# The last expert group of a two-layer transformer kernel: its filler matmuls set one matrix later, and its scatter split in two halves

## The chip, the cores and the metric

The kernel runs on one core of a Trainium2 chip. The metric is the device time of one launch in microseconds (us), lower is better. Everything is float32. A core has TensorE (PE, matmuls), VectorE (DVE), ScalarE (ACT), GpSimd (POOL) and SyncE (SP), which here issues the transfers.

## The reference

Two layers of a transformer on 256 tokens of width 1024. Each layer has an attention part (three branches, merged and projected) and a mixture of experts, and only the experts matter here:

```python
def hier_moe(h, w_grp, b_grp, w_router, b_router, w_gate, w_up, w_down):
    ...
        a = jnp.einsum('cd,edf->cef', t, w_gate)
        u = jnp.einsum('cd,edf->cef', t, w_up)
        hid = (jax.nn.silu(a) * u * combine[..., None]).astype(t.dtype)
        return jnp.einsum('cef,efd->cd', hid, w_down)
```

There are 32 experts of width 256, and a token uses two. The result is added to the residual x; the second layer is followed by a final normalization.

## The kernel before

**Stages.** Each layer is an attention block and a block of experts. The experts are handled in 8 groups of four. An expert has room for 32 tokens (`CAP`), so four experts fill the 128 columns of the array, each in its own strip of 32, and their four matmuls run side by side. An expert has three matrices of 1 MB each: gate, up and down. SyncE loads them one after another into a ring of 20 slots of SBUF, a load waiting only for the last reader of its slot.

**One group g in TensorE's program** (`moe_tensor`): `gate_up` (L1935) waits for the eight gate and up matrices of the group and issues its matmuls at L1947; `gather` (L1909, matmuls at L1919) collects the tokens of the next group; `turn_hidden` (L1979) transposes the hidden values, which ACT (L2080) and DVE (L2232, L2237) have made from the result of `gate_up` and which DVE takes back at L2245; `turn_weights` (L1971, L1976) transposes the selection weights, taken by ACT at L2084 into `ST`; `down` (L1985, L1996) multiplies by the down matrices, in two halves n of 512 output columns, into banks 5 and 6; ACT copies each half out of its bank into `ysb` (L2098); `scatter_group` (L2002, matmuls at L1954) adds the half of each expert's rows back to the tokens, in four accumulators in banks 0 to 3, one for each pair of token half t and column half.

**The end of a layer.** For the last two groups the order is another one: the down matrices of group 6 land behind the gate and up matrices of group 7, so `down` and `scatter_group` of group 6 stand behind `gate_up` and `turn_hidden` of group 7. Then come `turn_weights`, `down` and `scatter_group` of group 7. The down matrices of group 7 are loaded as halves (`down_half`, issued at L1803 and L1805 once `gate_up` of group 6 has read its slots, recorded as L594): first the four halves for n = 0, then the four for n = 1, and `down` of group 7 waits for the latter on the semaphore `s_side` (L1993). Each of the four last scatter sums is counted by `s_fin`, on which DVE adds it to the residual (L2255). In the second layer ACT then squares it for the final normalization (L807), and in the first layer the next attention block begins (its first matmuls are at L963).

**Fillers.** `keep_warm` (L596) issues matmuls of 128 columns on the identity, whose result nobody reads. A float32 matmul is two MATMUL records in the trace. In `gate_up` of the last group, twelve such fillers (`TAILWARM`, L49) stand between the wait for the sixth landed matrix (i = 5) and that for the seventh (i = 6):

```python
                pe.wait_ge(s_hde, g)
                for i in range(8):
                    if g == NGRP - 1 and i == 6:
                        keep_warm(pe, TAILWARM, bank[5])
                    moe_wait(pe, place(g, i))
```

TensorE works through its program in this order: a wait holds up everything behind it.

Of the kernel before, what the change touches and what calls it, by code (L numbers as in the profile page):

```python
# [39 lines left out]
NGRP = NE // 4  # L40
# [5 lines left out]
RING = 8  # L46
HROWS = 47
WARM, FILL = 14, 8
TAILWARM = 12  # L49
LOADS = 12 * NGRP  # L50


# [84 lines left out]
def program(nc, A, out, ctx):  # L137
# [195 lines left out]
    def csem(name):  # L333
        first[name] = sem(name)
        return first[name]
# [102 lines left out]
    s_hde = csem("expert_hiddenT_ready")  # L438
# [25 lines left out]
    def in_extra(c):  # L464

        return SLOTS < c < AHEAD
# [7 lines left out]
    def place(g, i):  # L474

        if g == NGRP - 1 and i < 8:
            return LOADS - 16 + i
        return 12 * g + i + (8 if g == NGRP - 2 and i >= 8 else 0)
# [9 lines left out]
    def moe_slot(c):  # L488

        assert c != SIDE and not in_extra(c)  # L490
        slot = PERM[turn_of(c)]
        g, i = item(c)
        if g and i < 8:
            other = PERM[turn_of(c ^ 1)]
            return max(slot, other) if c % 2 else min(slot, other)
        return slot
# [5 lines left out]
    def moe_home(c):  # L502

        return EXTRA[c - SLOTS - 1] if in_extra(c) else ring[:, moe_slot(c), :]
# [91 lines left out]
    def keep_warm(pe, n, b):  # L596

        for _ in range(n):
            pe.matmul(b[:, 0:P], ident, ident, start=True, stop=True)
# [210 lines left out]
    for layer in range(DEPTH):  # L810
# [5 lines left out]
        def moe_wait(eng, c):  # L816

            if c == SIDE:
                eng.wait_ge(s_part, PART + (layer + 1) * 64)
            elif in_extra(c):  # L820
                eng.wait_ge(s_side, layer * 96 + 32)
            else:
                eng.wait_ge(landed[moe_slot(c)], turns_moe[layer, c] * 16)
# [956 lines left out]
        def hidden_rows(g):  # L1780

            return hidT if g < NGRP - 1 else Sel[:, 0]
# [63 lines left out]
        def moe_tensor(pe):  # L1846
# [88 lines left out]
            def gate_up(g):  # L1935

                pe.wait_ge(s_hde, g)
                for i in range(8):
                    if g == NGRP - 1 and i == 6:
                        keep_warm(pe, TAILWARM, bank[5])  # L1940
                    moe_wait(pe, place(g, i))
                for k in range(KD):
                    if k % 4 == 0:
                        pe.wait_ge(s_xge, 2 * g + k // 4 + 1)
                    for e in range(4):
                        lo, hi = moe_slot(place(g, 2 * e)), moe_slot(place(g, 2 * e + 1))
                        last = pe.matmul(bank[4][CAP * e:CAP * e + CAP, :].rearrange("p (a f) -> p a f", a=2),  # L1947
                                         XT[:, k, CAP * e:CAP * e + CAP],
                                         ring[:, lo:hi + 1:hi - lo, k * F:(k + 1) * F],
                                         start=(k == 0), stop=(k == KD - 1))  # L1950
                last.then_inc(s_gu, 1)

            def scatter(g, t, half):
                return pe.matmul(bank[2 * t + half][:, :], ST[:, t * P:(t + 1) * P],  # L1954
                                 ysb[:, 512 * half:512 * half + 512], start=(g == 0), stop=(g == NGRP - 1),
                                 skip_group_check=True)
# [14 lines left out]
            def turn_weights(g):  # L1971
                pe.wait_ge(s_sw, g + 1)
                if g + 1 < NGRP:
                    pe.wait_ge(s_xge, 2 * g + 3)
                for t in range(NT):
                    last = pe.transpose(bank[7][:, t * P:(t + 1) * P], Sw[:, t, :], ident)  # L1976
                last.then_inc(s_st, 1)
# [4 lines left out]
                    last = pe.transpose(bank[4][:, a * P:(a + 1) * P], hid[:, 1, a::2], ident)  # L1982
                last.then_inc(s_hdt, 1)

            def down(g):  # L1985
                pe.wait_ge(s_hde, g + 1)
                for i in range(8, 12):
                    moe_wait(pe, place(g, i))
                for n in range(2):
                    if n == 1 and g + 1 < NGRP:  # L1990
                        pe.wait_ge(s_xge, 2 * g + 4)
                    if n == 1 and g == NGRP - 1:
                        pe.wait_ge(s_side, layer * 96 + 96)  # L1993
                    for a in range(2):
                        for e in range(4):
                            last = pe.matmul(bank[5 + n][CAP * e:CAP * e + CAP, :],  # L1996
                                             hidden_rows(g)[:, a, CAP * e:CAP * e + CAP],
                                             moe_home(place(g, 8 + e))[:, a * D + 512 * n:a * D + 512 * n + 512],
                                             start=(a == 0), stop=(a == 1))
                    last.then_inc(s_y, 1)  # L2000

            def scatter_group(g):  # L2002
                pe.wait_ge(s_ste, g + 1)
                for half in range(2):
                    pe.wait_ge(s_ye, 2 * g + half + 1)
                    for t in range(NT):
                        last = scatter(g, t, half)
                        if g == NGRP - 1:
                            last.then_inc(s_fin, 1)
                if g < NGRP - 1:  # L2010
                    last.then_inc(s_scat, 1)

            for g in range(NGRP):
                if g == 3:
                    load_overflow(pe)
                if g == 0:
                    first_gate_up()
                else:
                    gate_up(g)

                if g + 1 < NGRP:
                    pe.wait_ge(s_S, g + 3)
                    if g + 1 == 3:
                        pe.wait_ge(s_h2, 2)
                    for t in range(NT):
                        gather(g + 1, t)
                turn_hidden(g)
                if g < NGRP - 1:
                    turn_weights(g)
                if g < NGRP - 2:  # L2030
                    down(g)
                    scatter_group(g)

            down(NGRP - 2)
            scatter_group(NGRP - 2)
            turn_weights(NGRP - 1)
            down(NGRP - 1)
            scatter_group(NGRP - 1)

        def moe_scalar(act):  # L2040
            act.wait_ge(s_xa, 4)
# [218 lines left out]
        with nc.Block() as block:  # L2260
            if layer == 0:
                block.sync(setup_sync)
                block.scalar(setup_scalar)
                block.gpsimd(setup_gpsimd)
                block.tensor(setup_tensor)
            block.sync(attention_sync)
            block.gpsimd(attention_gpsimd)
            block.tensor(attention_tensor)
            block.scalar(attention_scalar)
            block.vector(attention_vector)  # L2270
            block.sync(moe_sync)
            block.gpsimd(moe_gpsimd)
            block.tensor(moe_tensor)
            block.scalar(moe_scalar)
            block.vector(moe_vector)
# [171 lines left out]
```

## Time and profile before

| | us |
|---|---|
| three runs | 1031.17, 1033.25, 1034.21 |
| median of the three | 1033.25 |
| the profiled execution, its own time | 1034.22 |
| its span, first to last instruction | 1032.2 |
| PE busy | 950.6 (92% of the span) |
| DVE busy, ACT busy | 342.6, 229.8 |
| read from HBM | 291.56 MB, 285 GB/s over the span |
| mean granted clock of TensorE | 0.970 of full |

The span is shorter than the time by what lies around the instructions. A granted clock of 1.00 in a row is TensorE at 2.4 GHz, and 0.50 is 1.2 GHz; there are only these two levels. A timeline row has its start in us from the beginning of the span, its length, engine, line and operation, output and inputs, and in brackets the idle time of the engine before it and what ended that.

### The profile page before, as it was taken

To read this page: it belongs to the slowest core of one execution; us is meant where nothing else is said; L and a number is where in the kernel's file an instruction comes from. 1 tells how busy PE (TensorE), PEld (TensorE's weight loads), DVE (VectorE), ACT (ScalarE), POOL (GpSimd) and SP (SyncE) were. 2 spreads that over 40 slices of the span, in tenths; PEclk is the share of its full clock that TensorE was granted. 3 is DMA by queue.
4 is the path that set the end of the run, shared out by engine and by line. 5 is a ranking of instruction groups with operands and counts; after the bars stand their busy time and mean duration, and the time that the engine had idled before them with its cause. 6 is when DMAs were issued, how large, how long until landed. Compare 5 with 4: busy or idle time off the path is not lost. (4 is left out here: it accounts for less than half of the span.)

```text
span 1032.2 us, 13965 instructions
## 1 busy us (share of the span) xinstructions
PE 950.6 (92%) x5564; PEld 648.3 (63%) x5564; DVE 342.6 (33%) x996; ACT 229.8 (22%) x660; POOL 44.8 (4%) x91
## 2 busy tenths in 40 slices
PE   9999999999999997676899999999999999976675
PEld 8888778774587543333288887887746855432342
DVE  2521676772324111110031217677532331100112
ACT  1211364550010120000111015655400102000002
POOL 0300000000000000000021000000000000000000
PEclk9999999999999998888999999999999999988899
DMA  9975645439959999999998452436399599999995
GB/s 301 305 238 165 143 138 153 163 124 314 402 191 354 383 423 421 421 421 421 353 328 275 134 169 78 141 98 233 126 363 378 197 376 406 421 421 421 421 418 200
DMA packets 136887, 295.15 MB, mean 286 GB/s; under 512 B 14110, under 2 KB 101364, under 8 KB 115060
## 3 DMA queue, kind: packets, MB, share of 16 engines
q1 hardware_dynamic: 132368, 289.41, 76.0%
q10 hardware_dynamic: 4452, 4.81, 2.3%
q8 instruction: 46, 0.75, 0.3%
q14 instruction: 21, 0.17, 0.0%
HBM read 291.56 MB, written 2.64 MB: 285 GB/s over the span
## 5 line engine op out<-in xcount | busy, mean ns | idle before, releaser
L1947 PE MATMUL bank<-ring,tail 128*32 128x512 f32 x896 | 112.7, 661 | 54.9 <-DMA ring<-in_moe_w_up 50.8
L1116 PE MATMUL bank<-ring,tail 128*128 128x256 f32 x672 | 156.2, 383 | 0.2
L1116 PEld LDWEIGHTS bank<-ring,tail 128*128 128x128 f32 x672 | 124.2, 190 | 24.5 <-issue 8.3
L1947 PEld LDWEIGHTS bank<-ring,tail 128*32 128x32 f32 x896 | 32.2, 120 | 132.5 <-issue 132.5
L971 PE MATMUL bank<-tail,ring 128*128 128x256 f32 x512 | 112.8, 380 | 0.0
L971 PEld LDWEIGHTS bank<-tail,ring 128*128 128x128 f32 x512 | 96.5, 190 | 13.3 <-issue 0.4
L2232 DVE SCALAR_TENSOR_TENSOR tail<-tail,bank 128x256 f32<-128x256 f32 x16 | 6.7, 421 | 263.6 <-ACT tail L2080 263.6
L1249 PE MATMUL bank<-ring,tail 128*128 128x512 f32 x192 | 83.6, 593 | 0.0
L1420 ACT ACTIVATE ring<-ring,small 128x128 f32<-128x128 f32 (+1 forms) x128 | 56.6, 444 | 76.8 <-DVE small L1678 76.8
L1996 PE MATMUL bank<-ring,tail 128*32 128x512 f32 x480 | 58.7, 596 | 5.1 <-DVE tail L2245 3.6
L1249 PEld LDWEIGHTS bank<-ring,tail 128*128 128x128 f32 x192 | 36.0, 190 | 43.4 <-issue 43.4
L1954 PE MATMUL bank<-tail 128*128 128x512 f32 x128 | 59.2, 605 | 0.0
L1858 PE MATMUL bank<-ring,tail 128*128 128x256 f32 x256 | 57.2, 380 | 0.0
L2080 ACT ACTIVATE tail<-bank 128x256 f32<-128x256 f32 x16 | 6.1, 384 | 224.7 <-PE bank L1947 204.6
L977 PE MATMUL bank<-ring,tail 128*128 128x256 f32 (+2 forms) x320 | 53.6, 327 | 0.0
L977 PEld LDWEIGHTS bank<-ring,tail 128*128 128x128 f32 x320 | 49.6, 191 | 3.5
L1858 PEld LDWEIGHTS bank<-ring,tail 128*128 128x128 f32 x256 | 47.9, 190 | 6.1
L1954 PEld LDWEIGHTS bank<-tail 128*128 128x128 f32 x128 | 23.0, 189 | 36.4 <-issue 36.4
L1919 PEld LDWEIGHTS bank<-tail 128*128 128x128 f32 x320 | 36.5, 192 | 8.4 <-issue 8.4
L1919 PEld LDWEIGHTS bank<-tail,x_res 128*128 128x128 f32 x192 | 38.2, 287 | 4.7 <-issue 3.4
L1919 PE MATMUL bank<-tail,x_res 128*128 128x128 f32 x192 | 39.7, 363 | 1.1 <-DVE tail L2160 1.1
L1996 PEld LDWEIGHTS bank<-ring,tail 128*32 128x32 f32 x480 | 14.8, 109 | 37.9 <-issue 27.9
(307 smaller groups left out, 1035.2 us busy)
## 6 DMA issues: line engine op xcount, KB each, us to landing
ring<-in_moe_w_gate SPq DMA_DIRECT2D x56, 1024.0 KB, 21.4
ring<-in_moe_w_up SPq DMA_DIRECT2D x56, 1024.0 KB, 23.5
ring<-in_moe_w_down SPq DMA_DIRECT2D x52, 1024.0 KB, 14.6
ring<-in_w_in SPq DMA_DIRECT2D x48, 1024.0 KB, 8.3
ring<-in_w_out SPq DMA_DIRECT2D x8, 1024.0 KB, 10.6
ring<-in_moe_w_down SPq DMA_DIRECT2D x16, 512.0 KB, 15.9
ring<-in_moe_w_gate SPq DMA_DIRECT2D x14, 512.0 KB, 8.8
ring<-in_moe_w_up SPq DMA_DIRECT2D x14, 512.0 KB, 8.9
```

The costliest lines, as they stand in the source:

```text
L971: last = pe.matmul(dst, weight(k), hT[:, k, :], start=(k == 0), stop=(k == KD - 1))
L977: last = pe.matmul(dst, tokens[:, k, t * P:(t + 1) * P], weight(k), start=(k == 0), stop=(k == KD - 1))
L1116: last = pe.matmul(dst, tokens[:, k, :], weights[:, k, :], start=False, stop=(k == KD // 2 - 1), skip_group_check=True)
L1249: last = pe.matmul(bank[j % 4][:, :], oT[:, b, c, t * P:(t + 1) * P], wo[:, c, :], start=(c == 0), stop=(c == 3))
L1420: last = act.activation(pr, pr, ACT.Exp, scale=scale, bias=mx[:, c:c + 1], accum_out=sm[:, c:c + 1])
L1858: last = pe.matmul(bank[4 + i][:, t * T:(t + 1) * T], mixT[:, k, t * P:(t + 1) * P], w[:, k, :], start=(k == 0), stop=(k == KD - 1))
L1919: last = pe.matmul(b[:, (k % 4) * P:(k % 4 + 1) * P], rows_k, Sel[:, g % 2, t, :], start=(t == 0 and k % 4 == 0), stop=(t == NT - 1), skip ...
L1947: last = pe.matmul(bank[4][CAP * e:CAP * e + CAP, :].rearrange("p (a f) -> p a f", a=2), XT[:, k, CAP * e:CAP * e + CAP], ring[:, lo:hi + ...
L1954: return pe.matmul(bank[2 * t + half][:, :], ST[:, t * P:(t + 1) * P], ysb[:, 512 * half:512 * half + 512], start=(g == 0), stop=(g == NGR ...
L1996: last = pe.matmul(bank[5 + n][CAP * e:CAP * e + CAP, :], hidden_rows(g)[:, a, CAP * e:CAP * e + CAP], moe_home(place(g, 8 + e))[:, a * D ...
L2080: act.activation(hid[:, 0, :], bank[4][:, 0:F], ACT.Tanh, scale=0.5).then_inc(s_ge, 1)
L2232: s(dve.scalar_tensor_tensor(out=hid[:, 0, :], in0=hid[:, 0, :], scalar=1.0, in1=bank[4][:, 0:F], op0=ALU.add, op1=ALU.mult))
```

## The change

`TAILWARM` becomes 10, and the fillers of the last group stand between the wait for the seventh matrix (i = 6) and that for the eighth (i = 7). `down` and `scatter_group` take the halves that they are to do. For the last group TensorE now does down half 0, scatter half 0, down half 1, scatter half 1, where it did both halves of `down` and then both of the scatter. The other groups are as before. No other engine's program changes.

```diff
-TAILWARM = 12
+TAILWARM = 10
...
                 for i in range(8):
-                    if g == NGRP - 1 and i == 6:
+                    if g == NGRP - 1 and i == 7:
                         keep_warm(pe, TAILWARM, bank[5])
                     moe_wait(pe, place(g, i))
...
-            def down(g):
-                pe.wait_ge(s_hde, g + 1)
-                for i in range(8, 12):
-                    moe_wait(pe, place(g, i))
-                for n in range(2):
+            def down(g, ns=(0, 1)):
+                if ns[0] == 0:
+                    pe.wait_ge(s_hde, g + 1)
+                    for i in range(8, 12):
+                        moe_wait(pe, place(g, i))
+                for n in ns:
...
-            def scatter_group(g):
+            def scatter_group(g, halves=(0, 1)):
                 pe.wait_ge(s_ste, g + 1)
-                for half in range(2):
+                for half in halves:
                     pe.wait_ge(s_ye, 2 * g + half + 1)
...
-            down(NGRP - 1)
-            scatter_group(NGRP - 1)
+            for half in range(2):
+                down(NGRP - 1, (half,))
+                scatter_group(NGRP - 1, (half,))
```

## Rows read from the trace of the kernel before

**Rows 1.** The page's busy tenths in 40 slices of the span.

```profile
PEclk9999999999999998888999999999999999988899
DMA  9975645439959999999998452436399599999995
```

**Rows 2.** Timeline of all engines, end of the second layer, in order of time.

```profile
985.34 21.72 SPq L594 DMA_DIRECT2D ring<-in_moe_w_down  x8
...
991.60 2.92 PE L599 MATMUL bank<-cst 128*128 128x128 f32 x24 [2.10 <-DMA ring<-in_moe_w_up]
...
996.52 8.77 PE L1947 MATMUL bank<-ring,tail 128*32 128x512 f32 x64 [2.01 <-issue]
...
1006.22 0.42 DVE L2237 TENSOR_TENSOR tail<-tail,bank 128x256 f32<-128x256 f32 x1
...
1006.70 0.50 PE L1982 MATMUL bank<-cst,tail 128*128 128x128 f32 x2 [1.40 <-DVE tail L2237]
...
1014.55 1.93 PE L1996 MATMUL bank<-ring,tail 128*32 128x512 f32 x16
...
1016.60 0.60 ACT L2098 ACTIVATE tail<-bank 128x512 f32<-128x512 f32 x1 [1.56 <-PE bank L1996]
...
1017.14 1.92 PE L1996 MATMUL bank<-ring,tail 128*32 128x512 f32 x16 [0.66 <-DMA ring<-in_moe_w_down]
...
1018.99 3.70 PE L1954 MATMUL bank<-tail 128*128 128x512 f32 x8
1019.13 0.60 ACT L2098 ACTIVATE tail<-bank 128x512 f32<-128x512 f32 x1 [1.93 <-PE bank L1996]
...
1020.15 0.69 DVE L2255 TENSOR_TENSOR x_res<-x_res,bank 128x512 f32<-128x512 f32 x1 [12.49 <-PE bank L1954]
...
1022.73 0.69 DVE L2255 TENSOR_TENSOR x_res<-x_res,bank 128x512 f32<-128x512 f32 x1 [0.17 <-PE bank L1954]
```

**Rows 3.** The same view at the end of the first layer.

```profile
486.22 2.92 PE L599 MATMUL bank<-cst 128*128 128x128 f32 x24 [1.99 <-DMA ring<-in_moe_w_up]
...
491.17 8.77 PE L1947 MATMUL bank<-ring,tail 128*32 128x512 f32 x64 [2.03 <-issue]
...
509.20 1.92 PE L1996 MATMUL bank<-ring,tail 128*32 128x512 f32 x16
...
511.25 0.60 ACT L2098 ACTIVATE tail<-bank 128x512 f32<-128x512 f32 x1 [1.56 <-PE bank L1996]
...
512.00 1.92 PE L1996 MATMUL bank<-ring,tail 128*32 128x512 f32 x16 [0.87 <-DMA ring<-in_moe_w_down]
...
517.59 0.69 DVE L2255 TENSOR_TENSOR x_res<-x_res,bank 128x512 f32<-128x512 f32 x1 [0.17 <-PE bank L1954]
...
519.15 1.09 PE L963 MATMUL bank<-cst,x_res 128*128 128x128 f32 x8 [1.60 <-PEq L2260]
```

**Rows 4.** TensorE by stretch, second layer: length, busy, granted clock, DMA share, GB/s.

```profile
911.40:914.80 3.40, 0.00 (x0) 1.00 1.01 422
914.90:917.20 2.30, 0.00 (x0) 0.50 1.01 420
947.00:952.30 5.30, 5.29 (x28) 0.50 1.02 425
976.80:979.60 2.80, 2.80 (x16) 0.50 1.01 421
979.70:985.00 5.30, 5.30 (x52) 1.00 1.01 422
```

**Rows 5.** All engines by stretch: PE, PEld, DVE, ACT and POOL busy, clock, DMA.

```profile
994.50:996.50 2.00, 0.02 (x1) 0.01 (x1) 0.00 (x0) 0.00 (x0) 0.00 (x0) 1.00 1.00 418
996.80:1000.00 3.20, 3.20 (x20) 1.09 (x16) 0.00 (x0) 0.00 (x0) 0.00 (x0) 0.50 1.03 430
1000.30:1005.00 4.70, 4.70 (x48) 1.58 (x40) 0.00 (x0) 0.00 (x0) 0.00 (x0) 1.00 1.00 414
```

**Rows 6.** Timeline of TensorE: a `gate_up` at full clock, group 3 of the second layer.

```profile
892.50 7.07 PE L1947 MATMUL bank<-ring,tail 128*32 128x512 f32 x64
```

## The prediction, on record before the change ran

> **What bounds the kernel now.** I read the page first. Over the whole span TensorE is busiest, but its last ten slices show the DMA engines at nine tenths or more nearly throughout while the granted clock drops to eight tenths: the experts of the second layer run at the pace of their weights [rows 1]. The page's chain of waits covers only the last 8 us, behind the last group, so it says nothing on the part that changes. I therefore took the timeline of the last group in each layer, and asked of every start what released it.
>
> Three things are to be seen there. First, the last wait for weights: in the second layer down half 1 of the last group starts at 1017.14, after 0.66 us of idle ended by a DMA, and in the first at 512.00 after 0.87 us [rows 2, 3]. Second, everything behind it is a fixed chain: from that start to the start of the last residual add it takes 1022.73 - 1017.14 = 5.59 us, and 517.59 - 512.00 = 5.59 us in the first layer [rows 2, 3]. Third, the `gate_up` in front ran partly at half clock (1.2 GHz): 0.50 from 996.8 to 1000.0, 1.00 from 1000.3 on [rows 5], and it took 8.77 us against 7.07 us at full clock [rows 2, 6]. That loss of 1.7 us costs almost nothing now, since the 0.66 and 0.87 us of waiting follow it: without it the wait would only be longer. So the layer ends at "last weights landed + 5.59 us". Call that landing L: 1017.14 and 512.00. The halves were issued from 985.34 on, behind the end of `gate_up` of group 6 [rows 2], which the change doesn't touch, and the stream in front of them is saturated at 414 to 430 GB/s [rows 4, 5]. I leave L where it is.
>
> **Part one: the order of the four steps.** Before, scatter half 0 (four MATMUL records) stood between down half 1 and scatter half 1, and it covered ACT's copy of down half 1. Now it stands in front of down half 1.
> - When can scatter half 0 start? ACT's copy of half 0 starts 1016.60 - 1014.55 = 2.05 us behind the first matmul of down half 0, takes 0.60, and the handover to TensorE I take from another edge of the same kind: DVE ends at 1006.22 + 0.42 = 1006.64 and TensorE starts at 1006.70, so 0.06 [rows 2]. That gives 1014.55 + 2.71 = 1017.26, which is 0.12 behind L, so the DMA wait hides nothing of the scatter itself. In the first layer: 509.20 + 2.71 = 511.91, 0.09 in front of L [rows 3].
> - The scatter half takes four records. The adds behind the scatter follow at (1022.73 - 1020.15) / 3 = 0.86 us for each two records [rows 2], so 1.72 us. Down half 1 then starts at 1018.98 and 513.63, which is 1.84 and 1.63 us later than before.
> - Behind it: ACT's copy starts 1019.13 - 1017.14 = 1.99 us later, takes 0.60, the handover 0.06; scatter half 1 begins; its first add comes 1020.15 - 1018.99 = 1.16 us after it and the last 0.86 later. Together 1.99 + 0.60 + 0.06 + 1.16 + 0.86 = 4.67 us, against 5.59 [rows 2]. Each layer gains 0.92 us here: the matmuls that have been taken out, less the copy that they covered.
> - Sum: 1.84 - 0.92 = +0.92 us in the second layer and 1.63 - 0.92 = +0.71 in the first. As a formula, with d the shift of the end of `gate_up`: the layer changes by max(1.84 + d, 0) - 0.92 and max(1.63 + d, 0) - 0.92. The new order only pays where `gate_up` ends 0.9 (0.7) us earlier, and its best is -0.92 a layer.
> - The two adds and squares of column half 0 come earlier on DVE and ACT, which idle there (12.49 us before the first add [rows 2]): nothing. The wait for ACT's copy now holds up down half 1 behind it, counted above. The wait for `ST` moves ahead of down half 1; ACT turns the weights in front of its copy of half 0, which is waited for as well: nothing. No transfer is moved; SP waits in this stretch only for the end of `gate_up`.
>
> **Part two: the fillers.** They are released by the sixth landed matrix at 991.6, and `gate_up` starts with the eighth at 996.52 [rows 2]; two matrices of 1 MB in 4.92 us are 2.46 us each, as 418 GB/s gives too [rows 5]. So the fillers will be released at about 994.05 (488.7 in the first layer).
> - At full clock 24 records took 2.92 us, 0.122 each [rows 2]; 20 records take 2.43 and end at 996.48, just as the eighth matrix lands. Nothing would be lost, and the idle 2.01 us in front of `gate_up` would be gone. With the clock up, `gate_up` would take 7.07 instead of 8.77: d = -1.70 [rows 2, 6].
> - But the idle stretch in front of the fillers grows from 2.10 us to 2.10 + 2.46 = 4.56 us. What does the clock do in it? No row has a gap of that length. The nearest above is one of 5.8 us (911.4 to 917.2, ahead of `gate_up` of group 4): full for its first 3.4 us, then 0.50 with no work in it [rows 4]. The nearest below are the gaps of 2.10 and 2.01 us: the clock held through the first (the fillers behind it ran at the full-clock rate), and behind the second it was full to 996.5 and half from 996.8 [rows 2, 5]. A gap of 4.56 us lies nearer to 5.8, so I take it that the clock is at half by 994 or falls within the first microsecond of the fillers.
> - The Trainium skill ("TensorE: Matmul & The Clock Gate", section "Why this matters for your kernels") asks for no idle stretch over some 3 us between bursts of matmuls. By that rule this change gives up the clock that the fillers are there to hold. The trace agrees for the gaps above 5 us [rows 4], and disagrees below: the clock fell behind a gap of 2.01 us [rows 5]. By the page alone `gate_up` would have been at full clock before, which leaves the sum where it is, since that loss was hidden.
> - How long does it stay low once work resumes? Group 6: 2.8 us at least, and full 2.9 us after 976.80; group 5: 5.3 us; this `gate_up`: to about 1000.1, 3.6 us [rows 4, 5]. From 994.05 the clock rises between 996.9 and 999.4. At half clock I double the full-clock price of the array: 0.107 of the 0.122 us is a quarter of the 0.43 us of a 512-column record (0.86 / 2, part one), so 0.213 us a record, at most 0.244.
> - Rise at 996.9: 13.4 records at half clock, 6.6 at 0.122, fillers end at 997.7, and `gate_up` runs at full clock from there: it ends 7.07 later at 1004.8 instead of 1005.29, d = -0.5 (-0.8 if the clock falls only during the fillers). Rise at 998: fillers end at 998.2, d = 0. Rise at 999.4: fillers end at 998.3, 1.1 us of `gate_up` at half clock cost 0.55, d = +0.65; with 0.244 a record about +1.
> - I take the middle, d = 0: the fillers cost `gate_up` 1.7 us of start and give it back in clock.
>
> **Sum.** +0.92 + 0.71 = +1.63 us; bounds +0.03 (d = -0.8) and +3.63 (d = +1.0). The first layer's share counts in full, for the attention behind it starts when its last add is done (1.56 us from 517.59 to 519.15 [rows 3]) and TensorE is its bound [rows 1]. Against the profiled execution: 1034.22 + 1.63 = 1035.85. It stands 0.97 above the median of 1033.25, so against that: **1034.9**. Changes under 0.3% (3.1 us) can't be told from none here.
>
> **Rivals.**
> - **The clock holds.** The fillers run at full clock, `gate_up` starts at 996.5 and stays at full: d = -1.70. Then the layers change by 0.14 - 0.92 = -0.78 and -0.92, together -1.70: 1031.6. For it: the clock held through 2.10 us, and the DMA wait would then swallow scatter half 0. Against it: a gap of 4.56 us. Even this is not faster by 0.3%. Chance 0.13.
> - **The fillers don't raise the clock**, the slower side. If the clock, low at 994, stays low through all fillers and through as much of `gate_up` as before (3.6 us), `gate_up` is pushed back whole: it starts at 998.3, d = +1.75, and the layers change by +2.67 and +2.46, +5.1 us: 1038.4. It decides at d = +0.75 (sum +3.1). For it: group 5 worked 5.3 us at half clock [rows 4]. Against it: group 6 was at full after 2.9 [rows 4]. Chance 0.13.
> - **The seam between the layers loses its clock.** In front of scatter half 1 TensorE now idles 0.95 us, then works 1.7, then idles 1.6 us before the next attention [rows 3]. If that is enough for the clock to fall, up to 1.7 us is added (what a low start cost `gate_up`): 1036.6. Against it: the last group's gaps of 2.10 and 2.01 us with 2.92 of work between them were just enough, and this is less [rows 2]. Chance 0.05.
> - **The order does nothing**: landings come so late in most runs that both orders wait. It takes L 1.8 us later than in the trace; the fixed part then gives -1.84 with the clock as it is. Against it: both layers show 0.66 and 0.87 of slack only. Chance 0.05.
>
> **How the numbers follow.** The forecast has 0.64; of it some 0.05 lies above +3.1 us. Slower by over 0.3%: that, most of the second rival, and nothing else, 0.15. Faster by over 0.3% is in no case, 0.05 for what I have not seen. The rest, 0.80, is within 0.3%. The range reaches from the first rival, 1031.6, to just above the upper bound of the forecast, 1033.25 + 3.63 = 1036.9, plus some spread of a median of such runs: 1037.3.
>
> **What would show it.** Right: fillers at about 994, 20 records taking over 3 us; a granted clock of 0.50 somewhere between 993 and 998; `gate_up` starting later than 996.5 but taking near 7.1; down half 1 starting 1.6 to 1.9 us behind where it did, released by the scatter's line and not by a DMA; nothing on TensorE for 0.9 us in front of scatter half 1; last add about 0.9 later. Wrong: fillers in 2.4 us, or a DMA ending the wait of down half 1 in the changed kernel. That L moves with the change would make the whole sum wrong.

## The result, and the profile after

The changed kernel takes 1035.81 us (median of 20 runs, 1033.56 to 1038.62), the kernel before 1033.10 in as many runs (1031.17 to 1034.33): ratio 1.0029, 95% interval 1.0021 to 1.0037, so +2.7 us. The profiled execution of the changed kernel took 1036.64 us with a span of 1034.7, 2.4 and 2.5 above those of the kernel before.

The page's slices are nearly those of [rows 1]: the granted clock differs only in the last slice (8 for 9), and the DMA digits differ in a few slices:

```profile
PEclk9999999999999998888999999999999999988898
DMA  9975654449959999999997452436398699999994
```

The timeline of TensorE, last group of the second layer, in the changed kernel (it answers to [rows 2]; the line numbers are one higher in `down` and two higher in the programs of ACT and DVE):

```profile
994.28 2.47 PE L599 MATMUL bank<-cst 128*128 128x128 f32 x20 [3.19 <-DMA ring<-in_moe_w_gate]
996.68 7.07 PE L1947 MATMUL bank<-ring,tail 128*32 128x512 f32 x64
1005.17 0.50 PE L1982 MATMUL bank<-cst,tail 128*128 128x128 f32 x2 [1.41 <-DVE tail L2239]
1006.72 5.24 PE L1997 MATMUL bank<-ring,tail 128*32 128x512 f32 x32 [1.05 <-DMA ring<-in_moe_w_down]
1011.89 3.70 PE L1954 MATMUL bank<-tail 128*128 128x512 f32 x8
...
1015.74 1.93 PE L1997 MATMUL bank<-ring,tail 128*32 128x512 f32 x16
1018.53 1.95 PE L1954 MATMUL bank<-tail 128*128 128x512 f32 x4 [0.87 <-ACT tail L2100]
1020.42 1.92 PE L1997 MATMUL bank<-ring,tail 128*32 128x512 f32 x16
1023.15 1.96 PE L1954 MATMUL bank<-tail 128*128 128x512 f32 x4 [0.81 <-ACT tail L2100]
```

The same at the end of the first layer [rows 3]:

```profile
488.32 3.83 PE L599 MATMUL bank<-cst 128*128 128x128 f32 x20 [4.50 <-DMA ring<-in_moe_w_gate]
492.08 7.07 PE L1947 MATMUL bank<-ring,tail 128*32 128x512 f32 x64
...
501.00 3.64 PE L1997 MATMUL bank<-ring,tail 128*32 128x512 f32 x32
...
508.42 1.92 PE L1997 MATMUL bank<-ring,tail 128*32 128x512 f32 x16
511.21 1.95 PE L1954 MATMUL bank<-tail 128*128 128x512 f32 x4 [0.87 <-ACT tail L2100]
513.10 1.92 PE L1997 MATMUL bank<-ring,tail 128*32 128x512 f32 x16
515.83 1.96 PE L1954 MATMUL bank<-tail 128*128 128x512 f32 x4 [0.81 <-ACT tail L2100]
519.38 1.97 PE L963 MATMUL bank<-cst,x_res 128*128 128x128 f32 x16 [1.60 <-PEq L2262]
```

And the last residual add of each layer in DVE's timeline:

```profile
517.82 0.69 DVE L2257 TENSOR_TENSOR x_res<-x_res,bank 128x512 f32<-128x512 f32 x1 [0.17 <-PE bank L1954]
...
1025.14 0.69 DVE L2257 TENSOR_TENSOR x_res<-x_res,bank 128x512 f32<-128x512 f32 x1 [0.17 <-PE bank L1954]
```

ACT's copy of down half 0, from its timeline in the second layer:

```profile
1017.79 0.60 ACT L2100 ACTIVATE tail<-bank 128x512 f32<-128x512 f32 x1 [1.56 <-PE bank L1997]
```

The reader is to see four things. The wait "DMA ring<-in_moe_w_down" in front of down half 1, 0.66 and 0.87 us before [rows 2, 3], is gone: down half 1 now follows scatter half 0 directly. In its place there are two waits for ACT in each layer (0.87 and 0.81 us), in which TensorE idles. In the first layer the fillers ran for the most part at half clock (3.83 us for 20 records) and `gate_up` at full. In the second they ran at full clock (2.47), and instead `down` of group 6 did not: it waited 1.05 us for its own weights and took 5.24 us, where it took 3.64. TensorE by stretch shows the clock there, first layer then second (the second view with all engines: PE, PEld, DVE, ACT, POOL, clock, DMA share, GB/s):

```profile
488.40:491.20 2.80, 2.80 (x13) 0.51 1.01 421
```

```profile
994.30:996.70 2.40, 2.40 (x23) 2.28 (x23) 0.00 (x0) 0.00 (x0) 0.00 (x0) 1.00 1.03 430
996.80:1003.70 6.90, 6.90 (x64) 1.86 (x62) 0.00 (x0) 0.00 (x0) 0.00 (x0) 1.00 1.01 420
1007.00:1010.00 3.00, 3.00 (x16) 0.67 (x12) 0.00 (x0) 0.00 (x0) 0.00 (x0) 0.50 1.06 388
```

**A measure for the tail.** Two profiles differ in when the expert stream of a layer begins by more than the change does, so I count from the start of `gate_up` where the eighth matrix releases it. For late fillers I take instead their release by the seventh plus the 2.49 us that one matrix takes (993.00, 995.40, 997.89 are the releases by matrices six to eight in the run e5 below, 2.4 to 2.5 apart). "Tail" below is the time from the eighth matrix to the start of the last residual add. Before: 517.59 - 491.17 = 26.42 us and 1022.73 - 996.52 = 26.21 [rows 2, 3]. After: 517.82 - 490.81 = 27.01 and 1025.14 - 996.77 = 28.37. Together 2.75 us more, close to the +2.7 of the medians.

A tail also holds whatever makes the stream of weights late. The traces also record when each transfer landed, and so they give the time L itself, also where TensorE no longer waits for it. So a second measure is the time from the landing of the last weights to the start of the last residual add. Before it is 5.64 us in both layers (landings at 511.95 and 1017.09), after it is 6.27 and 7.80 (landings at 511.55 and 1017.34): together 2.79 us more. From the landing of the eighth matrix to that of the last weights it is 20.6 to 20.9 us in 22 of the 26 layers profiled; the exceptions are the first layers of e1 (22.4), e7 (22.3), e11 (22.0) and e10 (21.2).

### The profile page after: what moved, and what is told of

Its sections match the earlier page's. It is cut to its first block and busy times, and to the rows that moved or that the text cites. A ratio compares the mean times of both kernels' runs of the same rounds, so it can differ in the third digit from the quotient of the medians.

```text
span 1034.7 us, 13953 instructions
## 1 busy us (share of the span) xinstructions
PE 952.8 (92%) x5556; PEld 647.7 (63%) x5556; DVE 342.5 (33%) x996; ACT 229.6 (22%) x660; POOL 45.1 (4%) x91
```

## The experiments

Ratios are to the kernel before, from the same chip. The last two columns are from one profile each, first layer / second.

| run | what | ratio, 95% interval | tail, us | last landing to last add, us |
|---|---|---|---|---|
| before | | 1 | 26.4 / 26.2 | 5.64 / 5.64 |
| change | | 1.0029, 1.0021 to 1.0037 | 27.0 / 28.4 | 6.27 / 7.80 |
| e11 | the change again | 1.0021, 1.0010 to 1.0032 | 28.0 / 27.1 | 6.10 / 6.56 |
| e1 | order only | 1.0036, 1.0024 to 1.0048 | 30.1 / 27.4 | 7.81 / 6.86 |
| e2 | fillers only | 1.0003, 0.9994 to 1.0012 | 26.4 / 26.2 | 5.63 / 5.63 |
| e3 | old order, no fillers | 1.0001, 0.9992 to 1.0009 | 26.2 / 26.1 | 5.64 / 5.64 |
| e7 | new order, no fillers | 1.0030, 1.0018 to 1.0042 | 27.7 / 28.6 | 5.63 / 8.06 |
| e5 | new order, clock held | 1.0014, 1.0004 to 1.0025 | 26.8 / 26.8 | 6.01 / 6.16 |
| e8 | old order, clock held | 1.0012, 0.9999 to 1.0024 | 26.4 / 26.2 | 5.64 / 5.64 |
| e4 | quarters | 1.0005, 0.9992 to 1.0018 | 25.5 / 26.7 | 4.78 / 6.23 |
| e6 | quarters, clock held | 0.9989, 0.9977 to 1.0000 | 25.5 / 25.5 | 4.79 / 4.78 |
| e10 | e6 again | 0.9984, 0.9972 to 0.9996 | 26.0 / 25.5 | 4.79 / 4.78 |
| e9 | quarters and one piece more, clock held | 0.9986, 0.9976 to 0.9997 | 25.5 / 25.4 | 4.71 / 4.72 |

Three pairs differ in the order alone, and in each the new order is slower with intervals that don't overlap: the change and e2 (1.0021 to 1.0037, 0.9994 to 1.0012), e7 and e3 (1.0018 to 1.0042, 0.9992 to 1.0009), and e1 and the kernel before (1.0024 to 1.0048, against 1).

### Each part of the change by itself

**e1**, the new order with the fillers as before (against the changed kernel):

```diff
-TAILWARM = 10
+TAILWARM = 12
-                    if g == NGRP - 1 and i == 7:
+                    if g == NGRP - 1 and i == 6:
```

> Only the new order of the four steps; the twelve fillers stay behind the sixth matrix. Theory A (the order costs, by the chain as the changed kernel showed it: from the first matmul of down half 0 to the last residual add 2.79 + 1.89 + 4.72 = 9.40 us, against the landing of the last weights plus 5.59 us): where the end of gate_up stays as in the profile of before, +1.2 us in the second layer and +1.0 in the first; where gate_up runs at full clock the second down half 0 starts up to 0.7 us earlier and the layers change by about +0.5 and +0.4. In the mean of runs +1 to +2.2 us, ratio 1.001 to 1.002. Theory B (the order costs nothing and it is the fillers that cost 2.7 us): ratio 1.000.

Measured: 1.0036. The order alone costs as much as the whole change; theory B is out. It is also above what I expected. The second layer of the profile is as expected: `gate_up` took 8.77 us as before, and the last add came 6.86 us behind the last weights for 5.64, so +1.2. The first is not: `down` of group 6 waited 2.63 us for its own weights, which released it 11.6 us behind `gate_up` (501.31 - 489.70; 9.9 in e5 below), and then ran at half clock. Of this layer's tail of 30.1 us some 1.5 is the stream's and not the order's: the last weights, too, landed 22.4 us behind the eighth matrix, for 20.9. One profile can't tell how much of the median comes from either. From TensorE's timeline:

```profile
498.18 0.50 PE L1982 MATMUL bank<-cst,tail 128*128 128x128 f32 x2 [1.41 <-DVE tail L2239]
501.31 5.33 PE L1997 MATMUL bank<-ring,tail 128*32 128x512 f32 x32 [2.63 <-DMA ring<-in_moe_w_down]
```

**e2**, the fillers alone (against the kernel before):

```diff
-TAILWARM = 12
+TAILWARM = 10
-                    if g == NGRP - 1 and i == 6:
+                    if g == NGRP - 1 and i == 7:
```

> Only the ten fillers behind the seventh matrix; the old order of down and scatter. Theory A (whatever the fillers do to the clock is covered by the wait for the last weights, 0.66 and 0.87 us, in this order): within 0.5 us of before, ratio 0.9995 to 1.0005, with a shorter or no DMA wait ahead of down half 1. Theory B (the fillers cost): +2.7 us, ratio 1.0026.

Measured: 1.0003, no change. TensorE in the second layer:

```profile
991.54 2.47 PE L599 MATMUL bank<-cst 128*128 128x128 f32 x20 [3.42 <-DMA ring<-in_moe_w_gate]
993.94 7.07 PE L1947 MATMUL bank<-ring,tail 128*32 128x512 f32 x64
...
1003.98 5.00 PE L1996 MATMUL bank<-ring,tail 128*32 128x512 f32 x32 [1.05 <-DMA ring<-in_moe_w_down]
...
1012.76 3.79 PE L1996 MATMUL bank<-ring,tail 128*32 128x512 f32 x32
```

The same half-clock `down` of group 6 as in the changed kernel (5.00 us). It uses up the whole slack: both halves of the last `down` run through (x32, no DMA wait shown), but the tail stays at 26.2 us, and the last add still comes 5.63 us behind the landing of the last weights. What the new order pays in full, the old one hid. That is theory A.

**e3**, the kernel before with `TAILWARM = 0`.

> The kernel before without its twelve fillers in the last group. If the granted clock in the last gate_up is hidden by the wait for the last weights, as the prediction says, this changes little: gate_up starts at the same landing, runs at half clock for 3 to 5 us, costs at most 0.7 us more than in the profile of before, and the layer ends at the landing of the last weights plus 5.6 us: ratio 1.000 to 1.001. If the clock there is on the path, it costs 1 to 2 us a layer: ratio 1.002 to 1.004.

Measured: 1.0001. `gate_up` waits 7.25 us for its weights, takes 8.71, and the wait for the last weights is there as before:

```profile
993.50 8.71 PE L1947 MATMUL bank<-ring,tail 128*32 128x512 f32 x64 [7.25 <-DMA ring<-in_moe_w_up]
...
1011.47 1.92 PE L1996 MATMUL bank<-ring,tail 128*32 128x512 f32 x16
1014.04 1.92 PE L1996 MATMUL bank<-ring,tail 128*32 128x512 f32 x16 [0.64 <-DMA ring<-in_moe_w_down]
```

So in the old order the twelve or ten fillers of the last group, at either place or at none, are worth nothing that can be measured.

**e7**, the changed kernel with `TAILWARM = 0`.

> The new order with no fillers in the last group. Theory (last add = start of down half 0 plus 9.40 us; without fillers that start was 18.6 to 18.7 us behind the eighth matrix in the old order): last add 28.0 us behind the eighth matrix, against 26.8: +1.2 us a layer, ratio 1.002 to 1.003, the same as with the fillers at either place. If the ten fillers behind the seventh matrix are what hurts in the new order, ratio 1.000 to 1.001.

Measured: 1.0030, as expected, with `gate_up` at 8.98 and 9.90 us. In the first layer down half 0 started 18.24 us behind `gate_up` and the last add 9.41 behind that (508.12 to 517.53); in the second, with 9.90, the tail is 28.6. In the first layer the new order cost nothing: the last weights landed late, 22.3 us behind the eighth matrix, and the last add came 5.63 us behind them, as in the old order. That is the prediction's fourth rival ("The order does nothing"), in one layer of one profile. The three kernels with the new order, with the fillers at either place or without them (e1, the change, e7), have overlapping intervals.

### What remains with the clock held

**e5**, the changed kernel with fillers spread so that no idle stretch is long:

```diff
-TAILWARM = 10
+TAILWARM = 9
-                    if g == NGRP - 1 and i == 7:
+                    if g == NGRP - 1 and i in (6, 7):
                         keep_warm(pe, TAILWARM, bank[5])
...
             def turn_hidden(g):
+                if g == NGRP - 1:
+                    keep_warm(pe, 5, bank[5])
...
                     for i in range(8, 12):
+                        if g == NGRP - 2 and i == 11:
+                            keep_warm(pe, 3, bank[5])
                         moe_wait(pe, place(g, i))
```

> The changed kernel with more fillers, so that TensorE has no long idle stretch in the last group: nine behind the sixth matrix, nine behind the seventh, five ahead of the transposes of the hidden values, three ahead of the last down matrix of group 6. Theory (the new order costs even with the clock held, since down of group 6 can't start before its own weights, about 10.0 us behind the eighth matrix; from there 7.42 us to down half 0 and 9.40 to the last add, 26.9 us behind the eighth matrix, against 26.3 to 26.8 in the kernels with the old order): about +0.3 to +0.6 us a layer, ratio 1.0005 to 1.0015, and 1 to 2 us faster than the change. Rival (clock lost in the last group is not the reason for more than the first 1.6 us of the change's cost): ratio 1.0025 or more, as before.

Measured: 1.0014, as expected: still slower, but by less. TensorE, second layer:

```profile
997.89 7.07 PE L1947 MATMUL bank<-ring,tail 128*32 128x512 f32 x64 [0.21 <-DMA ring<-in_moe_w_up]
...
1007.83 3.64 PE L2001 MATMUL bank<-ring,tail 128*32 128x512 f32 x32 [0.28 <-DMA ring<-in_moe_w_down]
...
1015.25 1.92 PE L2001 MATMUL bank<-ring,tail 128*32 128x512 f32 x16
1018.05 1.95 PE L1954 MATMUL bank<-tail 128*128 128x512 f32 x4 [0.87 <-ACT tail L2104]
```

Everything here runs at its full-clock length, and `down` of group 6 still starts only 9.94 us behind `gate_up`, its wait ended by a DMA. That is the floor: 9.94 + 7.42 + 9.41 = 26.77 us, in both layers.

**e8**, the same fillers in the old order.

> The kernel before with the fillers that hold the clock. Control for the two others: in the old order the layer ends at the last weights plus 5.6 us, whatever the clock did: ratio 0.9995 to 1.0005, with a longer wait for the last weights (1.0 to 1.4 us) ahead of down half 1. If the clock counted, -0.5 us or more a layer, ratio 0.999 or less.

Measured: 1.0012 with an interval that just holds 1, above what I expected. The expectation about the trace held: tails 26.4 and 26.2, and the wait for the last weights is now the longest of all kernels:

```profile
1013.72 1.93 PE L2000 MATMUL bank<-ring,tail 128*32 128x512 f32 x16
1016.94 1.92 PE L2000 MATMUL bank<-ring,tail 128*32 128x512 f32 x16 [1.29 <-DMA ring<-in_moe_w_down]
```

Where its median's extra 1.3 us lies I can't say; by this profile not in the last groups. Against e5, which has the same fillers, the old order is 0.87 us faster (1033.58 to 1034.45), and the tails say 0.39 + 0.59 = 0.98. The intervals of the two ratios overlap, so the runs alone don't show this difference.

### A version that beats both

If only work that fits in front of the last landing helps, it has to be ready early and be short. **e4** keeps the old order, but makes down half 0 in two quarters of 256 columns in two banks, which ACT copies one by one, and scatters the first quarter ahead of the wait:

```diff
+                    if n == 0 and g == NGRP - 1:
+                        for q in range(2):
+                            lo = 256 * q
+                            for a in range(2):
+                                for e in range(4):
+                                    last = pe.matmul(bank[5 - q][CAP * e:CAP * e + CAP, lo:lo + 256],
+                                                     hidden_rows(g)[:, a, CAP * e:CAP * e + CAP],
+                                                     moe_home(place(g, 8 + e))[:, a * D + lo:a * D + lo + 256],
+                                                     start=(a == 0), stop=(a == 1))
+                            last.then_inc(s_y, 1)
+                        pe.wait_ge(s_ste, g + 1)
+                        pe.wait_ge(s_ye, 2 * g + 1)
+                        for t in range(NT):
+                            scatter_quarter(t, 0)
+                        continue
```

(ACT's two copies and the scatter of the second quarter, behind down half 1, accordingly.)

> The old order for the halves, but down half 0 of the last group in two quarters of 256 columns in two banks, each copied by ACT on its own, and the scatter of the first quarter ahead of the wait for the last weights, where TensorE idles 0.66 and 0.87 us. The copy of the first quarter (0.38 us by the 256-column copies of this trace) is done when the second quarter's matmuls end, so the scatter of 0.86 us fits into the idle time. Theory (only work that fits in front of the last landing helps; what stands behind the landing must still cover ACT's copy): the first quarter leaves the 5.59 us behind the landing, minus some 0.1 us of copy that is no longer covered: -0.6 to -0.8 us a layer, together -1.2 to -1.6 us, ratio 0.9985 to 0.999. Rival (the split costs more in instructions and handovers than it saves): ratio 1.000 or above.

Measured: 1.0005, nothing gained. The first layer did what was expected (tail 25.5). In the second `down` of group 6 took 5.26 us, mostly at half clock, and down half 1 started behind the landing of its weights. So **e6** adds the fillers of e5.

> The quarters with the same fillers. In the first layer of the earlier run of the quarters the last add came 25.8 us behind the eighth matrix (26.5 in the kernel before), in the second 27.0, where down of group 6 ran at half clock (5.26 us for 3.64). Theory: with the clock held both layers come to 25.8 or less: -0.7 us a layer, together -1.4, ratio 0.9987. Rival (the fillers delay as much as they save): ratio 1.000.

Measured: 0.9989 with an upper end at 1.0000, median 1031.44 against 1032.29. TensorE, second layer (`scatter_quarter` is L2022, down half 1 L2015):

```profile
1011.08 1.93 PE L2003 MATMUL bank<-ring,tail 128*32 128x256 f32 x32
1012.94 1.13 PE L2022 MATMUL bank<-tail 128*128 128x256 f32 x4
1014.42 1.92 PE L2015 MATMUL bank<-ring,tail 128*32 128x512 f32 x16 [0.35 <-DMA ring<-in_moe_w_down]
1016.27 1.13 PE L2022 MATMUL bank<-tail 128*128 128x256 f32 x4
1017.24 1.88 PE L1954 MATMUL bank<-tail 128*128 128x512 f32 x4
```

Here the scatter of the quarter doesn't idle for ACT's copy, it fits, and 0.35 us are left over. Behind the landing the rest runs through without a gap: the last add starts 4.74 us behind it (1014.42 to 1019.16) and not 5.59.

**e10** is e6 again and **e11** the change again, beside each other.

> The quarters with the clock held once more, on the chip on which the change itself runs beside it, since their interval touched 1. Theory: the tail gives 0.7 to 0.9 us a layer against before: ratio 0.998 to 0.999. If it was the spread of the runs: ratio 0.9995 or above.

> The change itself, as it was timed. Theory (the order costs, with what the clock does in the last group on top): ratio 1.002 to 1.0035; last add 27 to 28.5 us behind the start of gate_up in a layer where down of group 6 runs at half clock, 26.8 where it runs at full and gate_up starts as its matrix lands.

Measured: 0.9984 (0.9972 to 0.9996) and 1.0021 (1.0010 to 1.0032), both ratios as expected. The last add of e10 comes 4.8 us behind the last weights in both layers; its first tail is 26.0 only because those landed late. In this profile of the change the fillers ran in part at half clock in both layers (3.34 and 3.91 us for 20 records), and in the first `gate_up` lost 0.74 us as well (7.81). `down` of group 6 ran at full clock in both (3.64 us), so neither case of the expectation is met; the first tail, 28.0, has 1.2 us of late weights for group 6 in it (their landing is 11.1 us behind the eighth matrix). TensorE in the second layer:

```profile
993.98 3.91 PE L599 MATMUL bank<-cst 128*128 128x128 f32 x20 [4.39 <-DMA ring<-in_moe_w_gate]
997.82 7.07 PE L1947 MATMUL bank<-ring,tail 128*32 128x512 f32 x64
...
1006.74 3.64 PE L1997 MATMUL bank<-ring,tail 128*32 128x512 f32 x32
```

**e9** moves one piece more, the second quarter's scatter for the first token half, ahead of the last landing.

> The quarters with the clock held, and one more piece ahead of the last landing: the scatter of the second quarter for the first token half (0.43 us), in the 0.35 to 0.45 us that TensorE still idles there. Theory: everything behind the landing shrinks by the piece until ACT's copy of down half 1 is bare again (2.65 us from down half 1 to the last scatter half, against 2.82 now): at most 0.2 us a layer better than the quarters, last add 25.2 to 25.4 us behind the start of gate_up, ratio 0.9985 to 0.999. Rival (the copy of the second quarter isn't ready, or the landing is passed): last add at 25.5 or later, ratio as the quarters.

Measured: 0.9986, tails 25.46 and 25.38 against 25.54 and 25.45: a gain of 0.08 us a layer by the trace, less than the 0.2 at most that I expected, and the first tail lies outside 25.2 to 25.4. The DMA wait is now gone. No gain in the median (1031.60; e10 has 1031.51).

## Why the prediction was right, and where its sum was short

It said 1034.9, within 0.3%, slightly slower; 1035.81 lies in its range. The predicted step was +1.63 us and the measured one +2.7. The first layer went by the forecast's mechanism. That the total came so near is in part luck, for the second layer went another way: its fillers took 2.47 us, which the prediction had listed as a sign that it is wrong, and there its formula gives a gain where 2.16 us were lost.

- **"L is not moved": right.** From the start of `gate_up` to the release of down half 1 by its DMA it is 20.83 and 20.62 us before [rows 2, 3], 20.54 in e3's second layer (993.50 to 1014.04) and 20.59 in e8's (996.35 to 1016.94). In the changed kernel no wait shows it, but the landings do: 20.89 and 20.71 us from the eighth matrix to the last weights, for 20.87 and 20.66 before.
- **"The half clock in `gate_up` costs nothing now": right.** e2, e3 and e8 change the clock and the place of the fillers in the old order and leave the tail at 26.1 to 26.4 us. In all eight layers with the old order the last add comes 5.63 or 5.64 us behind the last weights.
- **"The order costs, because nothing covers ACT's copy": right in kind**; e1 and e7 show it with no help from the new fillers. The terms were too small. From down half 0 to scatter half 0 I had 2.71 us, and it is 2.79 (508.42 to 511.21); scatter half 0 to down half 1, 1.72, is 1.89; down half 1 to the last add, 4.67, is 4.72 (513.10 to 517.82). Together 9.40 for 9.10: 0.3 us a layer. I had taken records back to back and a handover of 0.06 us; a switch from the scatter to `down` costs 0.17, and the handover from ACT is 0.14 (1017.79 + 0.60 to 1018.53).
- **"d shifts everything behind `gate_up` by itself": this step failed.** `down` of group 6 has its own weights to wait for, which land about 10 us behind the eighth matrix. In the profile of before it started 7.42 us ahead of down half 0, at 1007.13 and so 10.61 us behind `gate_up`; e5's floor is 9.94. So no wait showed, and I let down half 0 come earlier with d without an end. It can't come more than 0.7 us earlier. The first rival (the clock holds, -1.70 us) therefore doesn't exist: e5 is that case, and costs 0.35 to 0.6 us a layer more than the kernel before.
- **The clock moved, it wasn't only lost ahead of the fillers.** The first layer went as forecast: fillers over 3 us, `gate_up` late by 1.3 us and at 7.07, so d = -0.43. The formula gives 1.63 - 0.43 - 0.92 = +0.28, the short terms 0.30 more, and +0.59 was measured. Where the fillers kept the clock (second layer), d was -1.79 and the formula gives -0.87. But behind the 1.4 us of waiting for the hidden values, which was there before too [rows 2], the earlier `gate_up` left a new wait of 1.05 us for weights, and there the clock fell: `down` of group 6 took 1.6 us longer. The floor took back 1.13 us (`down` of group 6 started 9.95 us behind the eighth matrix and not 10.61 - 1.79 = 8.82), the clock 1.60 and the short terms 0.30, which makes the +2.16 measured. I had not looked past `gate_up` for the clock.
- **The seam between the layers kept its clock**: the next attention starts 1.56 us behind the last add as before (517.82 to 519.38), and its 16 records of L963 take 1.97 us in both kernels.

The change's 2.7 us thus come to about 1.0 for the order itself (e5 against e8), and the rest is time lost on TensorE in front of it, which the old order hid behind the last weights. This split rests on profiles: the interval of e5 overlaps with that of the change and with that of e8. What the runs show is that the new order costs, with the fillers at either place and without them, and that moving or leaving out the fillers alone costs nothing that can be measured.

## What to carry to other kernels

A DMA wait of 0.7 us is room for 0.7 us of work that is ready, and no more. Before moving work into it, add up when that work's own input is there, and look at what it covered where it stood: a copy by another engine, and every slower stretch ahead of the wait that the wait had made free. When a step ahead gets faster, look for the next landing that it runs into, even one whose wait doesn't show yet.

## What I had not expected of the hardware

TensorE's clock could fall after quite short idle stretches. In the changed kernel's second layer it went to half at about 1007, after 7 us of matmuls at full clock, 1.41 us idle, 0.50 of work and 1.05 idle. In the same layer 3.19 us of idle in one piece ahead of the fillers had not lowered it, 4.50 in the first layer had. The Trainium skill ("TensorE: Matmul & The Clock Gate", section "Why this matters for your kernels") asks to avoid idle stretches over some 3 us; the row with 4.50 us agrees, and the rows around 1007 show that keeping each below that is not enough.

It doesn't fall there each time. In the first layer of e4 nearly the same stretches, 1.40 us idle, 0.50 of work and 1.02 idle, left `down` of group 6 at its full-clock length:

```profile
496.04 0.50 PE L1982 MATMUL bank<-cst,tail 128*128 128x128 f32 x2 [1.40 <-DVE tail L2263]
497.57 3.64 PE L2011 MATMUL bank<-ring,tail 128*32 128x512 f32 x32 [1.02 <-DMA ring<-in_moe_w_down]
```

So one profile doesn't say what the clock does in such a place in the next execution.
